# A two-block sequence model on one core: products of 512 moving columns, and half-width levels of a triangular inverse

## The reference, cut to what matters

```python
u1 = squared_relu(h @ w_up) @ w_down            # 2048 -> 8192 -> 2048, first block
parts = u @ w_in                                # second block: 17440 columns
# one of its mixers, the gated delta net, per chunk of 128 tokens and per head:
a = eye + where(strict, (kb @ k.T) * decay, 0)  # 128 x 128, unit lower triangular
sol = triangular_solve(a, rhs)
# another, "forget": a decayed attention with exp(b_t - b_s) between all tokens of a chunk
y = sum(gate * proj) @ w_out
x = layernorm(ALPHA * x + g2 * (squared_relu(mod(x) @ w_ff1) @ w_ff2))
```

## Time and profile before

| | us |
|---|---|
| median of 3 runs | 5103.45 |
| lowest and highest | 5100.71, 5108.52 |
| profiled execution | 5102.65 |
| span in its trace | 5101.1 |
| PE busy | 4379.8 (86%) |
| DVE busy | 2899.9 (57%) |
| ACT busy | 1532.6 (30%) |

### The profile page before, as it was taken

One profiled execution on the slowest core, in us unless ns is written; L12 is line 12 of the kernel. 1 busy time (PEld: TensorE's weight loads), 2 busy tenths in 40 slices (PEclk: granted clock), 3 DMA queues, 4 the chain that ended last, 5 costly groups with the idle time before them and its releaser, 6 DMA issues.

```text
span 5101.1 us, 70606 instructions
## 1 busy us (share of the span) xinstructions
PE 4379.8 (86%) x28352; PEld 3732.5 (73%) x28352; DVE 2899.9 (57%) x6099; ACT 1532.6 (30%) x2682; POOL 0.2 (0%) x4
## 2 busy tenths in 40 slices
PE   7598897899999999998877676666888897999997
PEld 7333232889999978898667666666754697999997
DVE  4746544566566442245477777777633475655654
ACT  4211111444444332242212222222100243444442
POOL 0000000000000000000000000000000000000000
PEclk9799998999999999998888888888998999999998
DMA  5354554556565544474611111111332463655653
GB/s 176 98 164 138 157 165 138 158 150 190 184 184 187 181 119 122 122 194 132 181 43 44 44 45 48 45 50 47 89 101 63 133 203 117 186 188 180 191 184 110
DMA packets 383061, 669.57 MB, mean 131 GB/s; under 512 B 43897, under 2 KB 77402, under 8 KB 382220
## 3 DMA queue, kind: packets, MB, share of 16 engines
q1 hardware_dynamic: 327168, 595.74, 39.3%
q10 hardware_dynamic: 55564, 69.31, 4.1%
HBM read 634.87 MB, written 29.46 MB: 130 GB/s over the span
## 4 chain that ended last, share of the span: by engine, by line
PE 63%; DVE 14%; ACT 2%; issue 2%; DMA 1%; ACTq 1%; DVEq 0%
PE acc L544 13%; PE acc L545 12%; PE acc L546 12%; PE acc L586 8%; PE bank L544 2%; PE bank L545 2%; PE bank L546 2%; PE bank L1644 2%; PE bank L1635 1%; PE bank L1642 1%; PE bank L2033 1%; ACT weights_hi L508 1%; DVE arena L1490 1%; DMA arena<-s_read 1%; PE acc L1459 1%
## 5 line engine op out<-in xcount | busy, mean ns | idle before, releaser
L523 DVE TENSOR_TENSOR weights_lo<-weights_ring,weights_hi 128x512 fp32r<-128x512 f32 x1600 | 1094.2, 691 | 1037.3 <-ACT weights_hi L508 1036.2
L508 ACT ACTIVATE weights_hi<-weights_ring 128x512 fp32r<-128x512 f32 x1600 | 993.1, 629 | 1096.7 <-PE acc L546 899.5
L545 PE MATMUL acc<-arena_halves,weights_hi 128*128 128x256 f32 (+2 forms) x3136 | 924.6, 295 | 0.0
L544 PE MATMUL acc<-arena_halves,weights_lo 128*128 128x256 f32 (+1 forms) x2944 | 869.3, 295 | 20.9 <-DVE weights_lo L523 11.1
L546 PE MATMUL acc<-arena_halves,weights_hi 128*128 128x256 f32 (+1 forms) x2944 | 868.5, 295 | 0.0
L544 PE MATMUL acc<-moving_halves,weights_lo 128*128 128x256 f32 (+1 forms) x2816 | 793.8, 282 | 70.7 <-DVE weights_lo L523 69.5
L546 PE MATMUL acc<-moving_halves,weights_hi 128*128 128x256 f32 (+1 forms) x2816 | 789.1, 280 | 0.0
L545 PE MATMUL acc<-moving_halves,weights_hi 128*128 128x256 f32 x2624 | 734.0, 280 | 0.0
L545 PEld LDWEIGHTS acc<-arena_halves,weights_hi 128*128 128x128 f32 x3136 | 601.9, 192 | 12.5
L544 PEld LDWEIGHTS acc<-moving_halves,weights_lo 128*128 128x128 f32 x2816 | 536.5, 191 | 78.4 <-DVE weights_lo L523 51.4
L544 PEld LDWEIGHTS acc<-arena_halves,weights_lo 128*128 128x128 f32 x2944 | 565.2, 192 | 34.6 <-DVE weights_lo L523 12.3
(11 more groups left out here) (410 smaller groups left out, 5081.9 us busy)
## 6 DMA issues: line engine op xcount, KB each, us to landing
weights_ring<-in_w_in SPq DMA_DIRECT2D x624, 256.0 KB, 2.7
weights_ring<-in_w_ff SPq DMA_DIRECT2D x512, 256.0 KB, 3.0
weights_ring<-in_w_ada SPq DMA_DIRECT2D x384, 256.0 KB, 3.0
weights_ring<-in_w_up SPq DMA_DIRECT2D x256, 256.0 KB, 3.0
weights_ring<-in_w_down SPq DMA_DIRECT2D x256, 256.0 KB, 3.3
weights_ring<-in_w_out SPq DMA_DIRECT2D x128, 256.0 KB, 3.1
weights_ring<-in_w_branch SPq DMA_DIRECT2D x96, 256.0 KB, 3.2
s_state<-arena ACTq DMA_DIRECT2D x36, 256.0 KB, 3.0
```

Of the source, the lines that this page charges most:

```text
L508: a.activation(whi, k.slot(g.ring0 + kc), ACT.Copy).then_inc(*s.made("scalar_done", "high", n))
L523: v.tensor_tensor(wlo, k.slot(g.ring0 + kc), whi.bitcast(F32), ALU.subtract).then_inc(*s.made("vector_done", "low", n))
L544: pe.matmul(g.out[m], wlo[:, cols], xhi, start=first, stop=False, skip_group_check=g.shared)
L545: pe.matmul(g.out[m], whi[:, cols], xlo, start=False, stop=False, skip_group_check=g.shared)
```

## The change

**Dense.** Groups with the new field `both` take four banks. Per block `m` PE makes a product of `weights_lo` with the 256 high columns (256 wide, as before), and one product of `weights_hi` with the high and low columns together, 512 wide. The low half's sum then stands in the upper 256 columns of the bank and is added at the evacuation. A chunk has 8 products and 8 weight loads where it had 12 of each; the moving columns stay 3072. In chunk 0 the wide product comes first. The two sums are added on the way out: in `w_down`, `w_out`, `w_ff2`, `w_out2` and `w_glu` by two dependent DVE instructions per block, in `squared_relu` and `read` by a copy of the small sum by ACT and an addition by DVE. In `squared_relu` the square now is one instruction of DVE with the positive part in it, the high half is a copy by ACT made one step later, and the low half comes last in a step of DVE. `w_in`, `w_in2a` and `w_branch` are not changed.

**Delta net.** Level 6 starts from an identity, so `xt` is I minus the mask and `x` is I minus the left product: four products instead of twelve, no copy by ACT, no copies of the identity. In levels 5 to 0 only the half of the columns that a level can change is multiplied (64 moving columns instead of 128) and subtracted (256 elements per partition instead of 512). The delta strand is two rounds shorter; the background is spread over 50 rounds.

**Forget.** The two tiles go in one instruction: four instructions of 128 columns per direction and level in place of eight of 64.

```diff
@@ places
-        self.x2_hi, self.x2_lo = a.take(KD, 512), a.take(KD, 512)
+        self.x2 = a.take(2, KD, 512)
+        self.x2_hi, self.x2_lo = self.x2[:, 0], self.x2[:, 1]
@@ plan
+                        both=lambda kc: pair(self.hid[:, kc, :]),
-            read(n, **x2(T))
+            read(n, both=lambda kc: self.x2[:, :, kc, 0:T], **x2(T))
+            elif g.both:
+                g.out = [at[m][:, :] for m in range(4)]
@@ split_tensor
-                pe.matmul(g.out[m], wlo[:, cols], xhi, start=first, stop=False, skip_group_check=g.shared)
-                pe.matmul(g.out[m], whi[:, cols], xlo, start=False, stop=False, skip_group_check=g.shared)
-                mm = pe.matmul(g.out[m], whi[:, cols], xhi, start=False, stop=last, skip_group_check=g.shared)
+                if g.both:
+                    sums = g.out[m].rearrange("p (h t) -> p h t", h=2)
+                    if kc:
+                        pe.matmul(g.out[m][:, 0:T], wlo[:, cols], xhi, start=False, stop=False, skip_group_check=True)
+                    mm = pe.matmul(sums, whi[:, cols], g.both(kc), start=kc == 0, stop=last, skip_group_check=True)
...
@@ add_to_residual
-        k.nc.vector.tensor_tensor(dst, dst, g.out[m], ALU.add).then_inc(*k.s.made("vector_done", "residual", g.name, 4 * g.index + m))
+        serial(k, v.tensor_tensor(dst, dst, small, ALU.add))
+        v.tensor_tensor(dst, dst, big, ALU.add).then_inc(*s.made("vector_done", "residual", g.name, 4 * g.index + m))
@@ squared_relu, square_high
+        v.wait_ge(*s.at("small", g.name, g.index, m))
+        v.tensor_tensor(tmp, tmp, sums(g, m)[0], ALU.add).then_inc(*s.made("vector_done"))
+        v.wait_ge(*s.now("vector_done"))
+        v.scalar_tensor_tensor(k.relu_sq[:, m, :], tmp, 0.0, tmp, ALU.max, ALU.mult).then_inc(
...
+        a.wait_ge(*s.at(*summed(g, m)))
+        a.activation(k.relu[:, m, :], sums(g, m)[1], ACT.Copy).then_inc(*s.made("scalar_done", "small", g.name, g.index, m))
+    if m:
+        a.wait_ge(*s.at("relu_sq", g.name, g.index, m - 1))
+        a.activation(k.hid[:, (4 * g.col + m - 1) % 32, 0:T], k.relu_sq[:, m - 1, :], ACT.Copy).then_inc(
@@ forget_vector
-        for j in range(2):
-            own(v.tensor_tensor(m0[:, j], mid[:, j], c0[:, j], ALU.subtract))
-            own(v.tensor_tensor(m1[:, j], c1[:, j], mid[:, j], ALU.subtract), *(ev("spans", level) if j else ()))
+        own(v.tensor_tensor(m0, mid, c0, ALU.subtract))
+        own(v.tensor_tensor(m1, c1, mid, ALU.subtract), *ev("spans", level))
@@ delta_tensor
+def level_columns(t, level, second):
+    return t.rearrange("p (b two n) -> p b two n", two=2, n=P >> (level + 1))[:, :, second, :]
+    for j in range(NT):
+        mm = pe.matmul(b0[:, P * j:P * j + P], mt[:, j, :], k.ident, start=True, stop=True)
+    mm.then_inc(*s.made("tensor_done", *ev("left", 6)))
-                pe.matmul(b0[:, P * j:P * j + P], xt[:, j, :], y[:, j, :], start=True, stop=True)
+                pe.matmul(b0[:, 64 * j:64 * j + 64], xt[:, j, :], level_columns(y[:, j, :], level, r), start=True, stop=True)
@@ delta_vector
-    own(v.tensor_copy(x, idb))
-    own(v.tensor_copy(xt, idb))
-    for level in range(6, -1, -1):
+    own(v.tensor_tensor(xt, idb, mt, ALU.subtract))
+    yield
+    yield
+    v.wait_ge(*s.at(*ev("left", 6)))
+    own(v.tensor_tensor(x, idb, tiles(b0), ALU.subtract))
+    for level in range(5, -1, -1):
@@ heads2_tensor, heads2_vector, heads2_scalar
-        beside(lockstep(strands), 56, background(k, head, whole_tensor))
+        beside(lockstep(strands), 50, background(k, head, whole_tensor))
```

120 lines of the change are left out of this document (82 added, 38 removed).

## The result

The changed kernel takes 5037.85 us (median of 4 executions, 5035.96 to 5042.16) against 5105.99 (5100.71 to 5114.74): a ratio of 0.9866, 95% interval 0.9849 to 0.9883. It is faster, by 68 us in the medians and 64 us between the two profiled executions (5102.65 and 5038.51). The forecast was 98 us less, 5006. The time lies inside the range, near its upper end, and a third of the forecast gain is missing.

A forecast was written before the change was run, and what follows sets the result against it. PE was taken to bound the feed-forward stages and the heads, with DVE close behind in heads. Dense 33 + 28 - 7 = 54 us plus heads 44 made 98 us off 5102.65: 5005, forecast as 5006, range 4965 to 5045.

The forecast's parts named there:

- Arena stages: Dense products with tokens in `arena_halves` (`w_down`, `w_ff2`, `read`): 624 chunks at 53.3 ns less each, 33.3 us gained.
- the 346.7 ns a block: In `w_down`, `w_ff2` and `read`, a block falls from 360.0 ns to 120.0 + 226.7 = 346.7, 13.3 ns less.
- Moving stages: Dense products with tokens in `moving_halves`: 25 us from the stall, 2.6 us from `w_out2`, together 28 us.
- the stall that goes: PE waiting for split weights in `w_up` and `w_ff1`; shorter DVE steps save 0.84 us in each of 30 groups.
- the merging itself gives nothing: In `moving_halves` stages a block of 113.3 + 226.7 = 340.0 ns equals three products of 113.3: no gain at that speed.
- Rival (a): Dense products: a wide one is no cheaper than two narrow; dense gives 18 to 35, time 5041 or 5024; chance 0.15.
- Tails: Unhidden evacuation after `w_glu`, `w_out`, `w_down`, `w_out2`, `w_ff2`: two dependent instructions per block cost 1.45 us more each, 7 us lost.
- Heads: Delta net, eight heads: net 5.5 us a head, mostly from the shorter level 6, 44 us gained; bounds 3 and 8.
- 1.5 us for half-wide subtractions: In a head, four DVE subtractions of 0.6 become 0.34 where DVE is in the chain, and again at level 0.
- The 1.4 us taken off for the last rounds: In a head, background finished five rounds earlier leaves less to fill the last rounds, where strands wait: 1.4 us lost.
- the rule against it: Dense products: the Trainium skill's N / 2.4 + 2.5 ns makes a saved product worth 2.5 ns, 12 us in all.
- wide products at 220: Upper bound for dense products, wide ones having the `w_up` products' overhead: 50 us in arena stages, 43 in moving stages.

## Why the prediction was right and wrong

**Arena stages, 33 us forecast, 23 measured.** 16 groups of `w_down` and `w_ff2` fell from 46.08 to 44.81 on average, 20 us, and `read` by 0.43 in each of seven, 3 us. The step that failed is the 346.7 ns a block. It added a narrow distance out of a stream of narrow products and a wide one out of a stream of wide ones; in turn they make 347.7 or 352.5. The mechanism, fewer products, is right; its size was put half as high again as it is.

**Moving stages, 28 us forecast, 2 lost by measurement.** `w_up` and `w_ff1` gained 1.3 us in all, and `w_glu` and `w_out`, which had no stall and stood at 113.3, lost some 3 (groups of `w_out` from 21.76 to 22.60; but `w_out` took 22.61 with narrow products too, so this loss isn't surely the merging's). The prediction gave 25 us to the stall that goes. It goes: a DVE step takes 1.73 us, PE waits for nothing, and with three narrow products a group does take 21.76. The step that failed is "the merging itself gives nothing". It put 113.3 + 226.7 = 340.0 ns for a block, again two distances out of streams of one width, and the wide one moreover from tokens at a multiple of 128 bytes. Measured are 353.1, 13 ns more, 0.84 us a group, by chance the very size of the stall.

Of the 13 ns, the turns of narrow and wide make 6: with four of a width in a row a block takes 347.3. The other 7 would fit the place, where wide products alone go at 228.9 or 233.3 in place of 226.7, and narrow ones at 113.3 or 117.8. But the place isn't the whole answer: moved to a multiple of 128, where the streams of one width make 120.0 + 226.7 = 346.7, `w_up` still takes 353. Why a mixed stream is slower than the sum of its parts stays open.

The prediction named just this as what would make it wrong, wide products after narrow ones at another speed. Rival (a), overhead that belongs to columns and place in memory, comes nearest for these stages, but it let the stall's 25 us come and had a wide product cost no more than two narrow ones, where it costs more. Its 5041 met the 5038 by luck: it had 18 us for the dense part and 44 for the heads, against 9 and 55 in the traces.

**Tails, 7 us lost forecast, about 10 measured.** Timeline of DVE at the end of `w_out` in the changed kernel, to be set beside the earlier trace rows:

```profile
1032.20 0.42 DVE L672 TENSOR_TENSOR residual<-residual,bank 128x256 f32<-128x256 f32 x1 [4.59 <-PE bank L556]
...
1035.01 0.42 DVE L673 TENSOR_TENSOR residual<-residual,bank 128x256 f32<-128x256 f32 x1
```

Eight instructions, of which the first and the last are shown: 3.2 us, as worked out. The step that failed is that one row, that of `w_out`, was carried over to all five ends. At `w_glu` the price is 2.7 us (38.50 for 35.80) and at `w_out2` 3.3 (71.95 for 68.66), not 1.45; at the other three ends it is some 1.2 to 2.2, once the groups' own change is taken off. At `w_out2` the multiplying additions end 1.7 us later behind the start of the group than before. The other 1.6 are on PE, in the 32 products that follow them (L2181 before, L2257 now), shown as windows with the columns of the earlier trace rows, before and after:

```profile
4278.51:4285.67 7.16, 7.14 (x32) 5.96 (x32) 0.00 (x0) 0.00 (x0) 0.00 (x0) 1.00 0.01 2
4221.81:4230.66 8.85, 8.83 (x32) 7.15 (x32) 0.00 (x0) 0.00 (x0) 0.00 (x0) 0.81 0.01 2
```

The same products take 8.85 us for 7.16, with a granted clock of 0.81 for 1.00. Before, PE had stood for 1.07 us ahead of them, now for 2.80. With the old evacuation it stands for 1.08, the products take 7.16 at clock 1.00, and all of the 3.3 us is back. So a longer tail can be paid for twice, in the additions and in the clock of what follows; the prediction had no term for the second.

**Heads, 44 us forecast, 55 measured.** Timeline of DVE in head 2, to be set beside the earlier trace rows: second mask of level 6, second of level 5.

```profile
2842.39 0.69 DVE L1775 TENSOR_TENSOR arena<-arena,consts_sb 128x512 f32<-128x512 f32 x1
...
2846.97 0.69 DVE L1784 TENSOR_TENSOR arena<-arena,consts_sb 128x512 f32<-128x512 f32 x1
```

4.6 us later, where it was 9.6 and "about 4" was forecast. From the load of the head's state (2819.08 before, 2801.80 after) the pairs of level 5 end at 58.0 us before and at 53.2 now: 4.8 us, for 5.4 forecast, and the run with level 6 undone gives it 4.6. That PE wouldn't gain from 64 columns was right. The term mis-sized is DVE's: 1.5 us for half-wide subtractions, counted at the two places where DVE stood in the chain before. The run with whole columns gives 2.5. With level 6 out of the way PE would have come to the next levels so early that DVE's round bounds them, at places where the old chain had none of it; the half columns kept that from happening. The 1.4 us taken off for the last rounds were not seen.

**The sum.** 23 - 2 - 10 + 55 - 3 (the stretch ahead of `w_glu`) = 63 of the 64 us measured. The heads came out 11 us above their term and the dense part with the stretch ahead of `w_glu` some 45 below. That the time fell inside the range is in part luck: with the 44 us forecast for the heads it would have been 5049, past the upper end of 5045. Two slips on the way change nothing: the groups have 1280 chunks, so the rule against it gives 13 us and not 12, and with wide products at 220 the moving stages come to 28 + 17 = 45 and not 43.

## What to carry to other kernels

Merging two products of one weight tile into a wide one pays only where the wide product's own distance, in that place and between those neighbours, is under the two it replaces: measure it there, and don't add distances from streams of one kind. The place of a moving operand is worth a try by itself, since 64 bytes were worth 1 to 6% of a product here, in either direction, in streams of one width. Ask of a longer tail how long PE stands in it, and read the granted clock behind it. When one engine's round gets shorter, ask again at every later round which engine comes last, since work that was hidden can take its place.
